# RWKV half step in another order: raw scores earlier, k and b scores a step ahead, substitution ahead of the k product

## The chip, the cores and the metric

The kernel runs on one core of one Trainium2 chip. The metric is the device time of one execution in microseconds; all times below are microseconds unless marked otherwise. TensorE multiplies, VectorE and ScalarE read its results out of PSUM, GpSimd works on SBUF alone, SP (SyncE) issues most DMAs.

## The reference, cut to what matters

One layer of a trunk over 128 context and 512 latent tokens: a norm, an input projection, RWKV-7 time mixing and gated linear attention in both directions, an output projection, a mixture of experts, a final norm. The change lies in RWKV alone:

```python
def rwkv_scan(r, w, k, a_vec, b_vec, v, s0, reverse):
    def step(S, inp):
        r_t, w_t, k_t, a_t, b_t, v_t = inp
        sa = jnp.einsum('bhvk,bhk->bhv', S, a_t)
        S = S * w_t[:, :, None, :] + sa[..., None] * b_t[:, :, None, :] + v_t[..., None] * k_t[:, :, None, :]
        return S, jnp.einsum('bhvk,bhk->bhv', S, r_t)
```

## The kernel before

The scan is done in chunks of 64 tokens. A step h is 128 tokens (two chunks, one on each half of the partitions) of one direction d, for 8 heads of 64; there are NS = 10 steps (five tiles of 128 tokens, two directions, p, d = divmod(h, 2)). Within a chunk the recurrence becomes a triangular system of 64x64 per head. Its inverse X is grown: the 8x8 blocks of the diagonal are inverted by substitution on GpSimd (`inverse_of_eights`), travel through DRAM to be spread over the partitions, and then three rounds on TensorE double them: Z = U X, then X grows by X^T Z (jobs Z8 and X16, Z16 and X32, Z32 and X64, each with a transposed X: X8t, X16t, X32t).

The work of a step is spread over four iterations of one loop, H = -3 to 9, written out by hand for every engine. An iteration (a half step) works on four steps at once, and this text keeps the names of the code: H itself (state work: WU, G, seq, Y), s = H+1 (the inversion), o = H+2 (factors of k and r), l = H+3 (raw scores L, whose blocks GpSimd inverts one iteration later). The jobs of TensorE in it:

- L(l): raw scores, 32 instructions of 64x64, copied out by ScalarE (`raw_blocks`), stored by SP (`blocks_out`). Needs VectorE's `a_and_b(l)`.
- k(s): scores of k, 32 instructions of 64x128, read out by VectorE (`masked_k`). Needs VectorE's `r_and_k(s)`, which needs GpSimd's `k_product(s)`, which needs ScalarE's `k_factors(s)`. b(s): scores of b, read out by VectorE (`masked_b`).
- tK, tB, tA: transposes, copied out by ScalarE. tB being done frees g.b for GpSimd's `b_product(l)`.
- Z8, X16, Z16, X32, Z32, X64: the rounds. Z and the transposed X are copied out by ScalarE, the X by VectorE (`grown`, a sum). AV: masked k scores times v (`scored_v`). `masked_a(s)` (VectorE) makes the three masked copies of the raw scores that the Z products read.
- WU(H) needs X64(H) summed; G(H) (`chunk_maps`) needs WU; seq and Y (`state_from_...`, `rows_from_...`) carry the state and make the output rows. Y is copied out by ScalarE (`first_rows`) for the first direction to reach a token tile, and added by VectorE (`added_rows`) for the second: steps 1, 6, 7, 8, 9.

Every engine takes its instructions in the order written. Three things order them across engines: semaphores of single steps; `filled`, which counts the jobs of TensorE; and the banks. There are NB = 8 banks of PSUM, and a job uses the bank of its number in the list `jobs` modulo 8. `open_bank` and `open_early` (lines 403 and 1912 to 1927) make TensorE wait until the job eight places earlier in the list is drained, that is, read out by VectorE or ScalarE; a pair of jobs (two banks) waits for both ahead of its first instruction, except WU and the transposes, which open one at a time. So the list fixes, besides the order, whose reader each job waits for.

The lines that matter: the list at 353 to 363; `b_product`, `k_product`, `inverse_of_eights` and their loop at 820 to 862; ScalarE's loop at 1149 to 1187; VectorE's at 1697 to 1732; TensorE's at 2447 to 2491. In the profile all matmuls have line 1907, all transposes 1911, all of ScalarE's operations 907; VectorE's lines are 1558 (`masked_a`), 1573 (`masked_k`), 1566 (`masked_b`), 1582 (`grown`), 1590 and 1591 (chunk maps), 1536 and 1539 (`a_and_b`), 1544 to 1549 (`r_and_k`), 1600 (`next_state`), 1611 (`added_rows`).

## Time and profile before

| | us |
|---|---|
| median of 3 runs | 1030.03 |
| lowest, highest | 1026.69, 1031.54 |
| the profiled execution | 1028.65 |
| its span | 1026.8 |

| engine | busy us | share of the span |
|---|---|---|
| TensorE, matmul | 882.8 | 86% |
| TensorE, weight load | 543.9 | 53% |
| VectorE | 578.1 | 56% |
| ScalarE | 312.3 | 30% |
| GpSimd | 144.9 | 14% |

The span is from the first to the last instruction; the execution's own time is 1.85 longer. Weight loads overlap matmuls, so the two TensorE rows don't add. The granted TensorE clock is 0.92 of full speed in the mean. The loop of half steps runs from about 437 to 684; the start of it (half steps -3 to 0) is bound by waits from engine to engine, from then on TensorE is busy most of the time.

### The profile page before, as it was taken

The page shows a single profiled execution, that of the slowest core. Times are in us where ns is not written, and L with a number is a line of the kernel's source. Part 1 is how long each engine was busy: PE and PEld are TensorE (multiplying, and loading weights), DVE is VectorE, ACT ScalarE, POOL GpSimd, SP SyncE. Part 2 cuts the span into 40 slices and gives each one's busy share as a digit, 9 for nine tenths or more (in the row PEclk, how much of TensorE's full clock was granted, in tenths as well). Part 3 has the DMA queues.
Part 4 walks back from the last instruction along what each step waited for, and adds up shares of the span by engine and source line. Part 5 has one row for each costly group of instructions (what it writes and reads, how often), then busy time and mean ns, then how long its engine had stood idle before and what let it go on. Part 6 is the DMA issues. An engine that isn't in the chain of part 4 may idle for free.

```text
span 1026.8 us, 21484 instructions
## 1 busy us (share of the span) xinstructions
PE 882.8 (86%) x8900; PEld 543.9 (53%) x8900; DVE 578.1 (56%) x968; ACT 312.3 (30%) x549; POOL 144.9 (14%) x295
## 2 busy tenths in 40 slices
PE   2799999996995899625988898889995799999996
PEld 0545455563653555425877787754565544444442
DVE  1524026689799268863655666578535144445457
ACT  3221110131000216464655665323121022232213
POOL 6000111103002000042333224000000110010031
PEclk9799999997998789658999999999995699999998
DMA  9800522222223230002121221196005679999957
GB/s 341 312 34 1 177 82 93 83 83 82 83 97 128 83 92 1 1 14 50 32 41 31 42 40 33 47 309 229 41 21 182 228 260 366 363 374 367 341 142 226
DMA packets 119760, 142.46 MB, mean 139 GB/s; under 512 B 49964, under 2 KB 85224, under 8 KB 119272
## 3 DMA queue, kind: packets, MB, share of 16 engines
q1 hardware_dynamic: 110824, 116.55, 34.6%
q0 software_dynamic: 3744, 13.63, 4.3%
q10 hardware_dynamic: 5088, 10.82, 2.8%
q8 instruction: 74, 1.21, 0.5%
q14 instruction: 30, 0.25, 0.1%
HBM read 122.99 MB, written 18.00 MB: 137 GB/s over the span
## 4 chain that ended last, share of the span: by engine, by line
PE 74%; DVE 14%; issue 5%; ACT 2%; DMA 2%; POOL 1%; SPq 1%; ACTq 0%; DVEq 0%; POOLq 0%
PE bank L1907 67%; PE bank L1911 7%; DVE rk_r L1354 3%; DMA region<-in_w_ada_dram 1%; ACT region L907 1%; DMA rk_r<-h_rows_dram,slot_tokens 1%; DVE region L1354 1%; DVE cl_b L1256 1%; POOL yg_b L814 1%; DVE vtok_b L1465 1%; DVE cl_b L1825 1%; DVE region L1896 0%; ACT ada_row_buffers L907 0%; ACT w_sb L907 0%; DVE kk_b L1463 0%
## 5 line engine op out<-in xcount | busy, mean ns | idle before, releaser
L1907 PE MATMUL bank<-region 64*64 64x64 f32 (+3 forms) x3904 | 406.4, 303 | 45.6 <-issue 29.2
L1907 PEld LDWEIGHTS bank<-region 64*64 64x64 f32 (+1 forms) x3904 | 236.1, 152 | 203.7 <-issue 189.8
L907 ACT ACTIVATE region<-bank 128x256 f32<-128x256 f32 (+3 forms) x216 | 97.9, 453 | 409.4 <-PE bank L1907 290.4
L1911 PE MATMUL bank<-ident,region 128*128 128x128 f32 (+2 forms) x403 | 69.8, 310 | 27.3 <-DMA scratch<-in_gla_gk_dram 12.6
L1907 PE MATMUL bank<-region,rk_r 128*128 128x512 f32 x176 | 80.1, 610 | 0.8 <-issue 0.8
L1911 PEld LDWEIGHTS bank<-ident,region 128*128 128x128 f32 (+2 forms) x403 | 51.4, 158 | 44.4 <-issue 28.1
L1877 DVE TENSOR_SCALAR region<-region 128x256 f32<-128x256 f32 x16 | 4.7, 294 | 100.4 <-ACT region L907 100.4
L1354 DVE SCALAR_TENSOR_TENSOR rk_r<-region,vec,rk_r 128x512 f32<-128x512 f32 x64 | 54.2, 847 | 2.3
L1907 PEld LDWEIGHTS bank<-region,rk_r 128*128 128x128 f32 x176 | 33.6, 196 | 39.7 <-issue 38.5
L1582 DVE TENSOR_TENSOR region<-bank,region 128x256 f32<-128x256 f32 x60 | 25.5, 425 | 47.6 <-PE bank L1907 46.3
L882 POOL DMA_INDIRECT rk_r<-h_rows_dram,slot_tokens x16 | 15.2, 949 | 245.3 <-PE bank L1911 131.9
L1907 PE MATMUL bank<-scratch,region 64*64 64x64 f32 (+1 forms) x688 | 42.9, 230 | 4.8 <-DVE region L1591 2.9
L1907 PE MATMUL bank<-vtok_b,region 64*64 64x64 f32 x928 | 43.5, 218 | 2.7 <-DVE region L1611 1.6
L1907 PE MATMUL bank<-region,scratch 64*64 64x128 f32 (+1 forms) x512 | 37.3, 425 | 7.2 <-DMA region<-in_w_ada_dram 6.4
L1907 PEld LDWEIGHTS bank<-scratch,region 64*64 64x64 f32 (+1 forms) x688 | 40.3, 143 | 5.0 <-issue 3.9
L828 POOL TENSOR_TENSOR region<-kk_b,region 128x512 f32<-128x512 f32 x10 | 12.9, 1288 | 212.6 <-DVE region L1694 103.8
L1907 PEld LDWEIGHTS bank<-vtok_b,region 64*64 64x64 f32 x928 | 40.3, 135 | 4.4 <-issue 2.6
L907 ACT ACTIVATE region<-region 128x256 f32<-128x256 f32 (+1 forms) x27 | 24.7, 915 | 44.7 <-DVE region L1371 43.9
L1907 PE MATMUL bank<-cl_b,ada_row_buffers 128*128 128x512 f32 x80 | 35.3, 594 | 0.1
L1907 PE MATMUL bank<-cl_b,rk_r 128*128 128x512 f32 x80 | 35.2, 592 | 0.0
L1907 PE MATMUL bank<-rk_r,ada_row_buffers 128*128 128x512 f32 x80 | 35.1, 592 | 0.0
L1277 DVE COPY ada_row_buffers<-bank 128x512 f32<-128x512 f32 x12 | 8.3, 691 | 44.7 <-PE bank L1907 44.5
(282 smaller groups left out, 1152.4 us busy)
## 6 DMA issues: line engine op xcount, KB each, us to landing
region<-in_moe_w_dram SPq DMA_DIRECT2D x38, 1024.0 KB, 10.0
region<-in_w_ada_dram SPq DMA_DIRECT2D x12, 2048.0 KB, 8.9
region<-in_w_in_dram SPq DMA_DIRECT2D x6, 2048.0 KB, 7.8
cl_b<-in_moe_w_dram SPq DMA_DIRECT2D x10, 1024.0 KB, 12.5
expert_rows_dram<-yg_b ACTq DMA_DIRECT2D x14, 512.0 KB, 6.9
region<-late_condition_dram SPq DMA_DIRECT2D x3, 1024.0 KB, 9.3
a_rows_dram<-region SPq DMA_DIRECT2D x20, 128.0 KB, 3.0
region<-inverse_rows_dram SPq DMA_DIRECT2D x20, 128.0 KB, 3.2
```

The source lines that it names most:

```text
L814: tell(pool.tensor_tensor(yg_b[:, :], yg_b[:, :], sgm, ALU.mult), s_sig)
L828: tell(pool.tensor_tensor(g.b, kkT[:, :, tok], aa[:, d, :, tok], ALU.mult), s_t1)
L882: pool.indirect_dma_start(out=xg[:, i % 3], out_offset=None, in_=h2_dram, in_offset=bass.IndirectOffsetOnAxis(ap=idx[:, e:e + 1], axis=0)) ...
L907: return act.activation(out, in_, func, **kw)
L1256: own(dve.tensor_tensor_scan(u, scanm[:, :], u, 0.0, ALU.mult, ALU.add))
L1277: out_of(dve.tensor_copy(adarow(n), bank(("ada", n))[:, :]), "ada", n)
L1354: own(STT(out, lat[:, i:i + GH, j:j + GW], tap(i, j), out, ALU.mult, ALU.add))
L1465: tell(STT(prod[:, i], rT[:, i], vec[:, vrk + i:vrk + i + 1], kT[:, i], ALU.mult, ALU.mult), s_bon)
L1582: out_of(TT(dst[:, hp::2], bank((n, h, hp))[:, 0:RC * HD].rearrange("p (h i) -> p h i", h=RC), src[:, hp::2], ALU.add), n, h, hp)
L1825: tell(STT(acc[:, t], x1[:, t], rstd[:, t:t + 1], fg, ALU.mult, ALU.mult), s_yout)
L1907: return pe.matmul(out, lhsT, rhs, start=start, stop=stop)
L1911: return pe.transpose(out, in_, ident[0:n, 0:n])
```

## The change

Four edits, all of order. No instruction is added or removed; the same products, masks, copies and DMAs are issued.

- TensorE: L(l) moves from behind Z32 to behind Y, ahead of X32. k and b are computed one iteration earlier, for o in place of s, between Z32 and X64. X8t goes ahead of Z8, and tB between Z8 and G.
- The list of jobs follows, so every job's bank and the job it waits for change.
- ScalarE's copies follow TensorE's order: tK ahead of WU, X8t ahead of Z8, L ahead of AV. `k_factors(o)` moves from the head of the iteration to behind Z16.
- GpSimd: `inverse_of_eights(o)` ahead of `k_product(o)`. VectorE: in iteration 1 alone `added_rows` goes ahead of X32's sum; its order is otherwise the same.

```diff
@@ the list of jobs
-            jobs += inside(s, pair("k", s)) + inside(H, pair("WU", H))
-            jobs += inside(s, [("tK", s)] + pair("b", s) + pair("Z8", s) + [("X8t", s)]) + inside(H, pair("G", H)) + last(H, "G")
-            jobs += inside(s, [("tB", s), ("tA", s)] + pair("X16", s) + pair("Z16", s)) + inside(H, [("seq", H, 0)])
-            jobs += inside(H if H < NS - 2 else -1, [("seq", H, 1)]) + inside(s, [("X16t", s)]) + inside(H, pair("Y", H))
+            o = H + 2
+            jobs += inside(s, [("tK", s)]) + inside(H, pair("WU", H))
+            jobs += inside(s, [("X8t", s)] + pair("Z8", s) + [("tB", s)]) + inside(H, pair("G", H)) + last(H, "G")
+            jobs += inside(s, [("tA", s)] + pair("X16", s) + pair("Z16", s)) + inside(H, [("seq", H, 0)])
+            jobs += inside(H if H < NS - 2 else -1, [("seq", H, 1)]) + inside(s, [("X16t", s)]) + inside(H, pair("Y", H)) + inside(l, pair("L", l))
             if H == 1:
                 jobs += [("st", 0), ("st", 1), ("s0",), ("mrow",)]
-            jobs += inside(s, pair("X32", s) + [("AV", s), ("X32t", s)] + pair("Z32", s)) + inside(l, pair("L", l)) + inside(s, pair("X64", s)) + last(s, "X64")
+            jobs += inside(s, pair("X32", s) + [("AV", s), ("X32t", s)] + pair("Z32", s)) + inside(o, pair("k", o) + pair("b", o)) + inside(s, pair("X64", s)) + last(s, "X64")
@@ GpSimd
                 if 0 <= H + 2 < NS:
+                    inverse_of_eights(H + 2)
                     k_product(H + 2)
-                    inverse_of_eights(H + 2)
@@ VectorE
+                if H == 1:
+                    added_rows(H)
                 if new:
                     grown("X32", s)
-                if back:
+                if back and H != 1:
                     added_rows(H)
@@ TensorE
                 if new:
-                    scores("k", s)
+                    turned("tK", s)
                 if back:
                     wu_rows(H)
                 if new:
-                    turned("tK", s)
-                    scores("b", s)
+                    turned_x("X8t", s)
                     times_u("Z8", s)
-                    turned_x("X8t", s)
+                    turned("tB", s)
...
                 if back:
                     rows_from_state(H)
+                if later:
+                    scores("L", l)
...
                     times_u("Z32", s)
-                if later:
-                    scores("L", l)
+                if next_:
+                    scores("k", o)
+                    scores("b", o)
                 if new:
                     grown("X64", s)
```

## Rows read from the trace of the kernel before

**Rows 1.** The page: busy time by engine, and the chain by engine.

```profile
PE 882.8 (86%) x8900; PEld 543.9 (53%) x8900; DVE 578.1 (56%) x968; ACT 312.3 (30%) x549; POOL 144.9 (14%) x295
...
PE 74%; DVE 14%; issue 5%; ACT 2%; DMA 2%; POOL 1%; SPq 1%; ACTq 0%; DVEq 0%; POOLq 0%
```

**Rows 2.** Stretches: from:to, length, busy of five engines, clock, DMA share, GB/s.

```profile
487.00:493.00 6.00, 6.00 (x161) 5.22 (x157) 2.21 (x6) 3.19 (x6) 1.80 (x2) 0.72 0.19 27
...
580.00:600.00 20.00, 17.95 (x598) 15.75 (x596) 12.13 (x23) 12.86 (x26) 6.61 (x19) 1.00 0.20 37
```

**Rows 3.** Timeline of TensorE, 584 to 615: start, length, what, count, [idle before].

```profile
584.06 0.69 PE L1907 MATMUL bank<-region,ada_row_buffers 64*64 64x64 f32 x32 [0.43 <-ACT ada_row_buffers L907]
...
586.41 1.16 PE L1907 MATMUL bank<-region 64*64 64x64 f32 x64
...
588.22 0.69 PE L1907 MATMUL bank<-region,ada_row_buffers 64*64 64x64 f32 x32 [0.65 <-ACT region L907]
...
590.13 2.31 PE L1907 MATMUL bank<-region 64*64 64x128 f32 x37 [0.39 <-issue]
592.36 0.66 PE L1911 MATMUL bank<-ident,region 128*128 128x128 f32 x4
592.95 1.16 PE L1907 MATMUL bank<-region 64*64 64x64 f32 x64
...
594.63 1.10 PE L1907 MATMUL bank<-region,scratch 64*64 64x128 f32 x32
...
598.86 0.63 PE L1907 MATMUL bank<-region 64*64 64x64 f32 x29
...
603.98 0.69 PE L1907 MATMUL bank<-region,w_sb 64*64 64x64 f32 x32 [0.43 <-ACT w_sb L907]
...
608.14 0.69 PE L1907 MATMUL bank<-region,w_sb 64*64 64x64 f32 x32 [0.64 <-ACT region L907]
...
614.22 1.10 PE L1907 MATMUL bank<-region,scratch 64*64 64x128 f32 x32
```

**Rows 4.** Timeline of VectorE over the same half step.

```profile
584.87 0.88 DVE L1582 TENSOR_TENSOR region<-bank,region 128x256 f32<-128x256 f32 x2 [1.92 <-PE bank L1907]
...
586.72 0.69 DVE L1549 TENSOR_TENSOR region<-region 128x512 f32<-128x512 f32 x1
589.02 0.88 DVE L1582 TENSOR_TENSOR region<-bank,region 128x256 f32<-128x256 f32 x2 [1.61 <-PE bank L1907]
589.94 1.76 DVE L1558 TENSOR_TENSOR region<-region,maskA 128x1536 f32<-128x1536 f32 x1
591.73 1.42 DVE L1573 TENSOR_TENSOR region<-bank,mask 128x512 f32<-128x512 f32 x2
593.76 0.88 DVE L1566 TENSOR_TENSOR region<-bank,mask 128x256 f32<-128x256 f32 x2 [0.62 <-PE bank L1907]
...
597.69 0.89 DVE L1582 TENSOR_TENSOR region<-bank,region 128x256 f32<-128x256 f32 x2
```

**Rows 5.** Timeline of ScalarE: X16t's copy, Z32's and L's copies, `k_factors`.

```profile
583.10 0.60 ACT L907 ACTIVATE ada_row_buffers<-bank 128x512 f32<-128x512 f32 x1 [2.92 <-PE bank L1911]
...
587.21 1.63 ACT L907 ACTIVATE region<-bank 128x256 f32<-128x256 f32 x4
588.88 2.08 ACT L907 ACTIVATE region<-region,small,vec 128x128 f32<-128x128 f32 x4
```

**Rows 6.** Timeline of VectorE in half step 6: `added_rows`.

```profile
626.19 0.88 DVE L1611 TENSOR_TENSOR region<-bank,region 128x256 f32<-128x256 f32 x2
```

**Rows 7.** Timeline of the loop's start: X32(0), last substitution for step 1, Z8(1), G(0).

```profile
475.20 0.69 PE L1907 MATMUL bank<-region,w_sb 64*64 64x64 f32 x32 [1.15 <-ACT region L907]
...
478.72 0.21 POOL L854 TENSOR_TENSOR ada_row_buffers<-ada_row_buffers,region 64x14 f32<-64x14 f32 x1
...
486.76 0.69 PE L1907 MATMUL bank<-region 64*64 64x64 f32 x32 [2.32 <-issue]
...
487.97 1.96 PE L1907 MATMUL bank<-region,scratch 64*64 64x128 f32 x32
```

More of the change, by code:

```diff
@@ L1151, in _ @@
                 back, new, next_, later = H >= 0, 0 <= s < NS, 0 <= o < NS, l < NS
-                if next_:
-                    k_factors(o)
+                if new:
+                    turned("tK", s)
                 if back:
@@ L1158, in _ @@
                 if new:
-                    turned("tK", s)
+                    turned_x("X8t", s)
+                    by_chunk("Z8", s)
                 if l == 1:
@@ L1164, in _ @@
                 if new:
-                    by_chunk("Z8", s)
-                    turned_x("X8t", s)
                     turned("tB", s)
@@ L1172, in _ @@
                     by_chunk("Z16", s)
+                if next_:
+                    k_factors(o)
+                if new:
                     turned_x("X16t", s)
@@ L1177, in _ @@
                     first_rows(H)
+                if later:
+                    raw_blocks(l)
                 if new:
@@ L1181, in _ @@
                     by_chunk("Z32", s)
-                if later:
-                    raw_blocks(l)
                 if s == NS - 1:
@@ L2447, in _ @@
             for H in range(-3, NS):
-                s, l = H + 1, H + 3
-                back, new, later = H >= 0, 0 <= s < NS, l < NS
+                s, o, l = H + 1, H + 2, H + 3
+                back, new, next_, later = H >= 0, 0 <= s < NS, 0 <= o < NS, l < NS
                 if new:
-                    scores("k", s)
+                    turned("tK", s)
                 if back:
@@ L2454, in _ @@
                 if new:
-                    turned("tK", s)
-                    scores("b", s)
+                    turned_x("X8t", s)
                     times_u("Z8", s)
-                    turned_x("X8t", s)
+                    turned("tB", s)
                 if back:
@@ L2463, in _ @@
                 if new:
-                    turned("tB", s)
                     turned("tA", s)
@@ L2478, in _ @@
                     rows_from_state(H)
+                if later:
+                    scores("L", l)
                 if H == 1:
@@ L2485, in _ @@
                     times_u("Z32", s)
-                if later:
-                    scores("L", l)
+                if next_:
+                    scores("k", o)
+                    scores("b", o)
                 if new:
```

## The prediction

> **What bounds the kernel now.** Read the page's busy table and its chain first: TensorE is busy 86% of the span and carries 74% of the chain that ended last [rows 1]. That is a mean over many stages, so read next the table of stretches, for the loop that the change touches (about 437 to 684 us): in a steady 20 us TensorE is busy 17.95, VectorE 12.13, ScalarE 12.86, GpSimd 6.61, at the full 2.4 GHz [rows 2]. TensorE leads, but 2 us are idle. Third, the timelines of TensorE and VectorE over one half step, which say who ends each idle time. With X32's start at 584.06 as zero, TensorE runs X32 0, Z32 and L together 2.35, X64 4.16, k, WU 6.07, tK 8.30, b and Z8 8.89, G 10.57, Z16 14.80, the next X32 19.92 [rows 3]. Its idle times are 0.43 ahead of X32 (ScalarE's copy of X16t), 0.65 ahead of X64 (ScalarE's copy of Z32) and 0.39 ahead of WU (VectorE's sum of X64) [rows 3]. The two that ScalarE ends are where the new order puts L, k and b. VectorE ends none of them but the last, so what must be read of it is how much time it has in hand where the new order puts a wait on it.
>
> The names: H is the half step's state work, s = H+1 the step being inverted, o = H+2, l = H+3.
>
> **Banks first.** Eight PSUM banks go round in the order of `jobs`, so a job waits until the job eight places earlier has been read out. I counted both lists. Before: Z8 takes over the banks of X64's second half and k's first, X8t that of k's second, tA and X16 those of b. After: WU's second half takes over the bank of k(o)'s first half, X8t that of k's second, and Z8 the two of b(o). k(o) and b(o) are read only by VectorE's `masked_k` and `masked_b`, and those stand where they stood, behind `grown("X64")` and `masked_a`. So k and b are computed earlier, but four banks stay shut until VectorE comes round, and TensorE now wants them at once.
>
> **Leg A, X32 to X64.** Removed: L (32 instructions). Added: k(o) and b(o). On full clock 32 instructions of 64x128 take 1.10 (G), of which some 0.05 overlap the next group: 1.05, and 32 of 64x64 take 0.55 (half of b and Z8) [rows 3]. k(o) needs `r_and_k(o)`, which VectorE runs behind X32's sum: it starts at 0.81 and the last product ends at 3.35 [rows 4]. Z32 would be over at 2.9, so k(o) waits, a new wait of 0.6. The hop from VectorE to TensorE is 0.23 from X64's sum (589.90) to WU and 0.28 from X16's (598.58) to Z16 [rows 3, 4]; the profile has none shorter than that among these, I take 0.2 as both have a bank to open besides. k at 3.55, b at 4.60, X64 at 5.15, where it stood at 4.16: +1.0. ScalarE's copy of Z32 (first at 3.15, now perhaps 0.8 later as L's two copies come ahead, four copies 1.63 [rows 5]) is done by 4.0, so the 0.65 does go, but under work and a wait that are longer. Bounds: 0.9 to 1.2.
>
> **Leg B, X64 to G.** Counted from X64's start at 588.22: its sum starts at 0.80, `masked_a` (1.76) at 1.72, `masked_k` (2 x 0.7) ends at 4.93, `masked_b` (0.88) no longer waits for TensorE and ends at 5.83 [rows 4]. TensorE: tK to 1.15, then idle until X64's sum, WU's first half 1.9 to 2.8, then idle until `masked_k`'s first half, about 4.35, WU's second half to 5.25, X8t to 5.85, Z8 when b's banks are free, 5.98, tB 6.53, G 7.12. Before it is 6.41 here and 6.08 two half steps on [rows 3]: +0.7 to +1.05, I take +0.9. This is also where k's old cover is missed: k had filled VectorE's time at X64's sum, of which only 0.39 showed.
>
> **Leg C, G to Z16.** Now 4.23, and already VectorE's: its four chunk-map operations and X16's sum end at 598.58, Z16 starts at 598.86 [rows 3, 4]. Moving tB ahead of G takes 0.55 from under this chain and so shortens nothing; at best the 0.3 behind the sum shrinks. -0.1, bounds -0.3 to 0.
>
> **Leg D, Z16 to X32.** L is now in front of X32: +0.55, and it covers X16t's copy: -0.43. +0.1. L's inputs (`a_and_b`) are ready long before in both orders.
>
> **GpSimd, SP, ScalarE.** Substitution ahead of the k product releases the inverse's store and loads one product earlier. In steady steps nobody waits for it: the inverse is in well before Z8. The k product now comes behind the substitution, but `b_product` starts earlier too, as tB does; by these shifts it ends about 2 us before `r_and_k` needs it. ScalarE's `k_factors` (4 x 0.52, 2.08) moves into an idle time of 2.92 ahead of X16t's copy [rows 5]. The queues of DMAs on SP keep their order; L's store goes a little earlier. All of this I cost at nothing in steady steps, with the bound of 0.5 a step if k's product is late.
>
> **Sum.** An ordinary half step: 1.0 + 0.9 - 0.1 + 0.1 = 1.9 longer, 22.2 for 20.3. Where the Y rows are summed by VectorE (two operations, 0.92 with their gap [rows 6]) ahead of `r_and_k`, leg A grows by that: 2.8. The H's in turn, each as the change at its X64:
> - H=-1: little lies between Z16 and X16t's copy there, so `k_factors` delays it, X32 by some 0.5 (475.20 now [rows 7]), and leg A adds 1.0: +1.5.
> - H=0: TensorE now stands 2.32 until the inverse lands at 486.76, 7.8 after the substitution's last operation ended [rows 7]. The inverse comes earlier, but Z8 at 475.7 + 5.15 + 5.98 = 486.8 is no earlier: VectorE takes the inverse's place. G stays at 488. Now the clock stood at 0.72 in the mean just there, G taking 1.96 for 1.10 [rows 2, 3, 7]; with the pause broken up, I let it stay high: -1.3 (bounds -1.6 to 0). Then D +0.1, and A with `condition_columns` ahead of `r_and_k`: +1.65. Together +0.5.
> - H=1: B, C, and D without a gap to cover (+0.55), A +0.7 as X32 to X64 is already longer there: +2.0.
> - H=2 to 5: 4 x 1.9 = 7.6. H=6 and 7: 2 x 2.8 = 5.6. H=8 has B and C alone: +0.8. H=9: nothing.
> 1.5 - 1.5 (swallowed by the 2.32) + 0.5 + 2.0 + 7.6 + 5.6 + 0.8 = 16.5. Behind the loop all shifts by it. The profiled execution took 1028.65 (its span 1026.8); 1045.2, so 1045. The median of the three runs lies 1.4 above that execution, which would make 1046.5; both lie well inside the range. By the legs' bounds (each -0.4 to +0.5 in seven half steps, start and clock -3 to +4) it is 1038 to 1053.
>
> **The rivals.**
> (1) The clock. The new waits break TensorE's work from X64 to Z8 into pieces: of about 5.3 some 2.3 are idle. Before, the 2.32 of idle ahead of 486.76 was followed by half clock (1.2 GHz) at a mean of 0.72 in the next 6 us, G taking 0.86 longer; with as much for the two transposes behind it I put a fall at 1.6 [rows 2, 3, 7]. If that came in each of 8 half steps: 8 x 1.6 = 13 more, 1058; in one or two, it is inside the forecast. For it: the sum of idle is the same. Against: it's in two pieces with WU between. The Trainium skill has this case (TensorE: Matmul & The Clock Gate, A second HAM failure mode: psum-queue depth-cycling): a kernel that cycles through PSUM banks idles shortly and often, and the clock swings. By that page it would be the 1058. The trace of before, with short waits in every half step at full clock [rows 2, 3], speaks against it so far.
> (2) Not slower: TensorE's order decides after all. If `masked_k` and `masked_b` were through before TensorE asks (the point: `masked_k`'s first half by 2.8 behind X64, where I have 4.2), the two gaps of 0.43 and 0.65 go in eight half steps, 8.6, and the clock's 1.3: 1019. VectorE's fixed 0.88 and 1.76 stand against it.
> (3) Between: the work in hand eats leg A but not leg B, 1.1 of gaps against 0.9 of bank waits, and the result is no change, 1029. It needs `r_and_k` 1 us earlier; its place behind X32's sum is fixed by the program.
>
> **How the numbers follow.** Forecast 1045 with 0.67, rival 1 with 0.16, rival 2 with 0.09, rival 3 with 0.08. A measurement of this kernel tells about 0.5% (5 us) from no change. Faster 0.09; same 0.08; slower 0.83. The range must leave out no more than 0.2: 1033 to 1058 leaves out the low rivals and little above.
>
> **What would show it.** After: X32 to X64 5.1 to 5.2, and k(o)'s group starting just behind L1549; no idle ended by ScalarE ahead of X32 and X64; two new idle times of TensorE behind X64, before each half of WU, 0.7 and 1.5; `masked_b` with no idle before it; VectorE idle less behind X64; masked_a to masked_a 22.2 in place of 20.2 to 20.5, 23 where rows are summed. It would be wrong if WU's halves follow each other (then banks don't bind), or if k starts right at Z32's end.

## The result, and the profile after

The changed kernel takes 1049.15 us (median of four runs, 1047.59 to 1051.12) where the kernel before took 1029.18 (median of four): a ratio of 1.0195, 95% interval 1.0163 to 1.0227. That is 20 us slower; the forecast was 1045, its range 1033 to 1058.

The page of the kernel after: busy time by engine, and the chain by engine.

```profile
PE 895.0 (85%) x8900; PEld 552.8 (53%) x8900; DVE 575.7 (55%) x968; ACT 312.4 (30%) x549; POOL 146.7 (14%) x295
...
PE 72%; DVE 16%; issue 3%; ACT 3%; DMA 3%; POOL 1%; SPq 1%; ACTq 0%; DVEq 0%; POOLq 0%
```

Against [rows 1]: the same 8900 matmuls are busy 12.2 us longer, and the chain gives VectorE 2 points more and TensorE 2 fewer. Now TensorE over the half step that answers to [rows 3] (start, length, what, count, idle time before and who ended it; X32 starts at 591.72).

```profile
591.72 0.69 PE L1912 MATMUL bank<-region,ada_row_buffers 64*64 64x64 f32 x32
593.62 1.15 PE L1912 MATMUL bank<-vtok_b,region 64*64 64x64 f32 x32 [1.21 <-DVE region L1585]
594.70 0.66 PE L1916 MATMUL bank<-ident,region 128*128 128x128 f32 x4
595.29 2.13 PE L1912 MATMUL bank<-region 64*64 64x64 f32 x96
597.42 0.69 PE L1912 MATMUL bank<-region,ada_row_buffers 64*64 64x64 f32 x32
598.05 0.66 PE L1916 MATMUL bank<-ident,region 128*128 128x128 f32 x4
599.22 1.09 PE L1912 MATMUL bank<-region 64*64 64x128 f32 x16 [0.51 <-DVE region L1585]
601.68 1.09 PE L1912 MATMUL bank<-region 64*64 64x128 f32 x16 [1.38 <-DVE region L1576]
602.71 0.66 PE L1916 MATMUL bank<-ident,region 128*128 128x128 f32 x4
603.42 0.69 PE L1912 MATMUL bank<-region 64*64 64x64 f32 x32
604.04 0.66 PE L1916 MATMUL bank<-ident,region 128*128 128x128 f32 x4
604.63 1.10 PE L1912 MATMUL bank<-region,scratch 64*64 64x128 f32 x32
```

X32 and X64 find their operands: no idle time ahead of either is ended by ScalarE here (in the last two half steps, which have no L, it still is: 0.43 and 1.32, 0.43 and 1.11). Behind X64 stand two idle times, 0.51 where the rows of before have 0.39, and a new one of 1.38; WU, one group of 32 before, comes in halves of 16, and the second waits for line 1576, `masked_k`. VectorE beside it, to be held against [rows 4]:

```profile
598.23 0.88 DVE L1585 TENSOR_TENSOR region<-bank,region 128x256 f32<-128x256 f32 x2 [3.17 <-PE bank L1912]
599.15 1.76 DVE L1561 TENSOR_TENSOR region<-region,maskA 128x1536 f32<-128x1536 f32 x1
600.94 1.42 DVE L1576 TENSOR_TENSOR region<-bank,mask 128x512 f32<-128x512 f32 x2
602.39 0.88 DVE L1569 TENSOR_TENSOR region<-bank,mask 128x256 f32<-128x256 f32 x2
605.85 0.43 DVE L1593 TENSOR_TENSOR region<-bank,identh 128x256 f32<-128x256 f32 x1 [2.58 <-PE bank L1912]
```

X64's sum, `masked_a`, `masked_k` and `masked_b` follow without a gap, and the second half of WU starts at 601.68, just as the first of `masked_k`'s two operations has ended (600.94 + 0.71). Then VectorE idles 2.58 for G.

In this half step AV came late, so k found its operands. Two half steps earlier it waited, 0.41; the trace names nobody, but line 1552, the last product of `r_and_k`, ends at 548.86, 0.10 ahead:

```profile
548.17 0.69 DVE L1552 TENSOR_TENSOR region<-region 128x512 f32<-128x512 f32 x1
548.96 1.57 PE L1912 MATMUL bank<-region 64*64 64x128 f32 x64 [0.41 <-issue]
```

**The ledger.** VectorE's sums mark the legs in every half step: A from X32's sum to X64's, B from X64's to the first chunk map, C to X16's, D to X32's. Between the first X64's sum and the tenth, nine steps:

| us | before | after | change |
|---|---|---|---|
| A, nine legs | 39.4 | 53.1 | +13.8 |
| B | 65.0 | 75.5 | +10.6 |
| C | 17.1 | 16.5 | -0.6 |
| D | 69.8 | 68.3 | -1.5 |
| nine steps | 191.2 | 213.4 | +22.2 |
| first X64's sum at | 480.2 | 478.1 | -2.1 |
| behind the tenth | 355.4 | 356.7 | +1.3 |

The three last rows make 21.4, the difference of the two profiled executions (1050.10 and 1028.65). The -2.1 is not the change's doing. GpSimd's first product of the loop, ahead of which the two kernels are the same, starts 2.8 earlier in the profiled execution after; from there to the first X64's sum it is 42.8 before and 43.5 after.

```profile
437.38 1.27 POOL L828 TENSOR_TENSOR region<-kk_b,region 128x512 f32<-128x512 f32 x1 [103.75 <-DVE region L1694]
434.62 1.27 POOL L829 TENSOR_TENSOR region<-kk_b,region 128x512 f32<-128x512 f32 x1 [103.67 <-DVE region L1697]
```

Leg B has two lengths. It is 6.48 in most half steps before; after, it is 7.62 at H = 2, 3, 5 and 7, and 9.0 at H = 0, 1, 4, 6 and 8. The second length is the clock. Of H = 4:

```profile
575.01 1.09 PE L1912 MATMUL bank<-region 64*64 64x128 f32 x16 [0.51 <-DVE region L1585]
577.48 1.97 PE L1912 MATMUL bank<-region 64*64 64x128 f32 x16 [1.38 <-DVE region L1576]
579.38 1.11 PE L1916 MATMUL bank<-ident,region 128*128 128x128 f32 x4
```

and in the table of stretches (clock behind the five busy times), this fall and the one of H = 6:

```profile
577.40:580.80 3.40, 3.32 (x32) 2.66 (x36) 1.56 (x4) 0.81 (x2) 0.00 (x0) 0.50 0.00 0
625.20:628.60 3.40, 3.40 (x51) 2.62 (x46) 1.11 (x3) 1.20 (x2) 0.00 (x0) 0.50 0.00 0
```

The idle times are the same 0.51 and 1.38 as at H = 5 above, but the second half of WU then runs at 1.2 GHz, 1.97 for 1.09, and the fall costs 9.0 - 7.62, about 1.36 of leg. Before, the loop had one fall (a stretch at a granted clock of 0.50) from 488.0 to 491.5 [rows 2]; after, five in these nine steps. So leg B's +10.6 is nine times 1.14 and five times 1.36, 17.1, less 6.6 by which four of its nine places had been longer than 6.48 before (9.86 at H = 0, with the wait for the inverse and the fall, and 8.93 at H = 8, with a pause of 2.06 of which more below).

### The profile page after: what moved, and what is told of

It is laid out like the page before. It is cut to its first block, busy times and chain, and to the rows that moved or that the text cites. A ratio compares the mean times of both kernels' runs of the same rounds, so it can differ in the third digit from the quotient of the medians.

```text
span 1048.3 us, 21494 instructions
## 1 busy us (share of the span) xinstructions
PE 895.0 (85%) x8900; PEld 552.8 (53%) x8900; DVE 575.7 (55%) x968; ACT 312.4 (30%) x549; POOL 146.7 (14%) x295
## 3 DMA queue, kind: packets, MB, share of 16 engines
q8 instruction: 74, 1.21, 0.5%
## 4 chain that ended last, share of the span: by engine, by line
PE 72%; DVE 16%; issue 3%; ACT 3%; DMA 3%; POOL 1%; SPq 1%; ACTq 0%; DVEq 0%; POOLq 0%
PE bank L1912 66%; PE bank L1916 7%; DVE rk_r L1357 3%; ACT region L908 2%; DVE region L1561 2%; DMA region<-in_w_ada_dram 1%; DVE region L1585 1%; DMA rk_r<-h_rows_dram,slot_tokens 1%; DVE region L1576 1%; DVE region L1357 1%; DVE cl_b L1259 1%; POOL yg_b L815 1%; DVE vtok_b L1468 1%; DVE cl_b L1830 0%; DVE region L1901 0%
## 5 line engine op out<-in xcount | busy, mean ns | idle before, releaser
L1912 PE MATMUL bank<-region 64*64 64x64 f32 (+3 forms) x3904 | 411.5, 309 | 60.1 <-issue 19.4
L1912 PEld LDWEIGHTS bank<-region 64*64 64x64 f32 (+1 forms) x3904 | 240.3, 156 | 222.6 <-issue 179.9
L1916 PE MATMUL bank<-ident,region 128*128 128x128 f32 (+2 forms) x403 | 73.4, 315 | 27.7 <-DMA scratch<-in_gla_gk_dram 12.7
L829 POOL TENSOR_TENSOR region<-kk_b,region 128x512 f32<-128x512 f32 x10 | 12.9, 1290 | 226.4 <-PE bank L1916 111.8
L1280 DVE COPY ada_row_buffers<-bank 128x512 f32<-128x512 f32 x12 | 8.3, 691 | 43.7 <-PE bank L1912 43.5
## 6 DMA issues: line engine op xcount, KB each, us to landing
region<-in_moe_w_dram SPq DMA_DIRECT2D x38, 1024.0 KB, 10.1
```

What stands on the lines that cost most here:

```text
L829: tell(pool.tensor_tensor(g.b, kkT[:, :, tok], aa[:, d, :, tok], ALU.mult), s_t1)
L1912: return pe.matmul(out, lhsT, rhs, start=start, stop=stop)
L1916: return pe.transpose(out, in_, ident[0:n, 0:n])
```

## The experiments

Each was read by its legs, by the waits of TensorE, and by its falls of the clock. "Stops" is TensorE's idle time in the nine steps that nothing in the trace ends ("issue" in the view of waits); what most of them are comes with the fourth group of runs.

| kernel | us | ratio to before, 95% | first X64's sum at | nine steps | falls in them | stops |
|---|---|---|---|---|---|---|
| before | 1028.2 to 1029.2 | | 480.2 | 191.2 | 1 | 12.9 |
| after | 1049.15 | 1.0195 (1.0163, 1.0227) | 478.1 | 213.4 | 5 | 8.7 |
| a_masks_early | 1039.91 | 1.0109 (1.0083, 1.0135) | 479.5 | 200.6 | 2 | 14.7 |
| a_rk_early | 1045.05 | 1.0175 (1.0156, 1.0194) | 482.2 | 202.8 | 1 | 6.6 |
| a_both_early | 1036.40 | 1.0076 (1.0047, 1.0104) | 484.8 | 194.6 | 2 | 10.2 |
| a_wu_twice | 1038.72 | 1.0103 (1.0058, 1.0148) | 478.9 | 200.8 | 1 | 6.8 |
| a_L_back | 1044.35 | 1.0158 (1.0118, 1.0199) | 483.1 | 203.5 | 0 | 10.5 |
| a_both_L_back | 1034.24 | 1.0059 (1.0035, 1.0082) | 481.4 | 197.4 | 2 | 13.1 |
| a_pool_undone | 1068.61 | 1.0393 (1.0355, 1.0430) | 483.7 | 225.7 | 7 | 8.0 |
| b_L_first | 1035.00 | 1.0068 (1.0045, 1.0090) | 480.0 | 197.6 | 2 | 12.0 |
| b_best | 1029.83 | 1.0005 (0.9989, 1.0021) | 481.0 | 191.9 | 1 | 16.7 |
| b_shift | 1025.78 | 0.9975 (0.9953, 0.9998) | 479.5 | 188.9 | 1 | 10.1 |
| b_tk | 1026.00 | 0.9982 (0.9962, 1.0002) | 480.4 | 185.7 | 0 | 12.0 |
| b_tk_rk | 1024.26 | 0.9955 (0.9933, 0.9978) | 478.6 | 187.0 | 0 | 12.8 |

The columns behind the ratio are of one execution each, and two of them carry a spread that is not the edits'. GpSimd's first product of the loop starts anywhere from 434.6 to 439.2, though all these kernels are the same up to there, and the first X64's sum moves with it. And the mean granted clock of the executions that make up a median differs as much as the falls could make it: 0.915 to 0.922 in the kernel after (the profiled one had 0.915), 0.917 to 0.927 in a_L_back (the profiled one 0.927), where five falls of 3.4 us at half clock are 0.008. How many falls the other executions had isn't known.

Stops counts short handovers between groups too, k's waits for `r_and_k` where the trace names nobody, and in the kernel before the 2.32 at 486.76 [rows 7], which was a wait for the inverse; the pauses in the middle of a group or over 0.25 that are none of these come to 5.4 there.

### The banks and `r_and_k`

```diff
 a_masks_early, against after (VectorE)
-    masked_a(s); masked_k(s); masked_b(s)
+    masked_a(s)
 ...
     r_and_k(o)
+    masked_k(o)
     grown("X64", s)
+    masked_b(o)
```

> The kernel after, with VectorE's masked_k of the next half step put ahead of X64's sum and its masked_b right behind that sum, so that WU's second half finds its bank read. Theory 1 (the banks cost leg B its 1.14 us per half step, and the idle that they break up costs the clock, 1.36 us in five half steps): leg B back to 6.5 us, the idle of 1.4 us before WU's second half gone, X64's sum later by at most 0.2; with nine half steps 8 to 10 us from the banks, and up to 7 more if no stretch of the loop falls to 1.2 GHz that did not fall before the change: 1033 us, between 1031 and 1041. Theory 2 (the clock falls for another reason, such as the waits of leg A): the 8 to 10 us from the banks alone, 1040, with the low clock still in five half steps. Theory 3 (the banks are not what is waited for: the order of TensorE itself costs the time): unchanged at 1049.

Measured 1039.9. What TensorE waited for in the nine steps, after and here (total, times, longest):

```profile
PE bank L1912 <- DVE region L1576: 12.4, 9, 1.4
PE bank L1912 <- DVE region L1585: 9.6, 17, 1.2
PE bank L1912 <- issue: 7.9, 13, 1.5
```

```profile
PE bank L1913 <- issue: 13.9, 27, 2.0
PE bank L1913 <- DVE region L1585: 9.3, 13, 0.9
PE bank L1913 <- ACT region L908: 7.0, 5, 2.3
PE bank L1917 <- issue: 0.8, 5, 0.2
```

The wait for `masked_k` was 9 x 1.38 = 12.4 and is gone; leg B is 6.13 in seven of its nine places, and only one fall stands behind an X64, at H = 7 (the other comes at 523.1 in leg A of H = 1). Theory 3 is out: the banks were waited for. Nine legs B give 75.5 - 56.6 = 18.9 back, yet the nine steps are only 12.8 shorter, as legs A and D got 6.1 longer and the stops rose from 8.7 to 14.7. In the medians 9.2 is left, half of what the banks, and the falls behind them, had cost in leg B. The time fits theory 1's upper end and theory 2's 1040 alike; what speaks for theory 1 is the falls, two for five, in one execution.

```diff
 a_rk_early, against after
 VectorE:  added_rows(1) / r_and_k(o) / X32's sum / other added_rows
 ScalarE:  k_factors(o) / growths_for_k(o) / X16t's copy
```

> The kernel after, with r_and_k of the next half step ahead of X32's sum on VectorE and the factor growths_for_k ahead of the copy of X16t on ScalarE, so that k's scores of the next half step don't wait for r_and_k. X32's sum can start later for it. Theory 1 (k's wait for r_and_k is 0.6 us of leg A, and 1.5 to 2.5 where added_rows or condition_columns stand ahead of it): the legs A of 4.95 to 5.1 fall to about 4.5, those of 5.7 to 7.5 to about 4.7; 6 to 8 us in all, 1042. Theory 2 (leg A is longer because TensorE has k's and b's scores in it, and r_and_k ends in time anyway): leg A stays at 5.0 and the time within 0.3% of the kernel after, 1049. Should r_and_k come too late for its new place, X32's sum waits for it and leg D grows by 0.5 or more: above 1049.

Measured 1045.05, 0.4% under the kernel after and between the two theories' 1042 and 1049. Where nothing else came in, leg A is 4.30 to 4.33 for 4.93 to 4.99: k's wait for `r_and_k` was 0.6 with its hop. Where it comes early, X32's sum waits for it: leg D is 7.62 nearly everywhere, and it was 7.0 in its shortest places. Theory 1 held for leg A; what it left out is that leg D pays the same 0.6. The nine steps are 10.7 shorter (7.0 in legs A, mostly at H = 0, 4, 6 and 7, and 5.5 in legs B, four falls fewer, against 1.8 more in D), but they begin 4.1 later; 2.1 of that lie ahead of the loop.

> Both edits in one: r_and_k ahead of X32's sum, masked_k ahead of X64's, masked_b behind it. If the two costs are separate (the banks on leg B, r_and_k on leg A) the gains add up: about 23 us less than the kernel after where the clock holds too, 1026 to 1030, level with the kernel before or a little under it; 1034 if the clock still falls in five half steps. If TensorE's order itself has a cost that no order of the other engines takes away, it ends above 1035 with the clock high.

Measured 1036.4. That is over the 1035 named for a cost of TensorE's order itself, but the clock fell twice. The best of its steps are 20.43 to 20.61, in TensorE's new order; the kernel before has 19.92 to 20.49. It lies 7.6 above before in the medians (1028.75) and 7.8 in the profiled executions. Of these, 4.7 are ahead of the first X64's sum, 1.0 of it ahead of the loop; between there and the sum the clock came up at 482.2 and not at 471.0 (the loop starts at 1.2 GHz in all of these kernels). 3.4 are in the nine steps, 2.4 of them in the one of H = 1, where AV waits 2.3 (below).

### The clock

```diff
 a_wu_twice, against after (TensorE): WU's first half is computed twice
+    for again in range(2 if j == 0 and h + 1 < NS else 1):
         for n in range(4 * j, 4 * j + 4):
```

> The kernel after, in which TensorE computes WU's first half twice while it waits for the bank of WU's second half (the repeated products are the same, nothing of the computation is left out). Sixteen more products of 64 rows take about 1.1 us, the idle ahead of the second half is 1.4. Theory 1 (the idle broken in two between X64 and Z8 is what makes the clock fall in five half steps): with the second idle filled, the loop's falls at this place go, 1.36 us each, and the time is about 1043 us; where the repeated products end after the bank is free they cost up to 0.2 each. Theory 2 (the falls hang on something else in the half step, such as the waits for r_and_k and the code loads): falls and time as in the kernel after, 1049 to 1051.

Measured 1038.7: work added, and 10.4 us gone. Leg B is 7.62 or 7.63 in six of nine places and long (9.69) only at H = 3, where the one fall of the nine steps stands, right behind a stop of 1.61; the kernel after had five. That agrees with the link: with TensorE at work between X64 and Z8 the falls went. But the edit also moves all later code, and it isn't only falls that went. The nine steps are 12.7 shorter: 4.3 in legs B (four falls of 1.36 are 5.4), 5.0 in legs A and 3.4 in legs D, which this edit doesn't touch and whose stops fell otherwise (s = 7: 5.85 for 7.52). The start and what lies behind take 2.1 back.

But the idle behind X64 isn't enough for a fall. a_rk_early (one fall) and a_L_back (none) keep all nine waits of 1.38; what they changed is work and waits in leg A. So what TensorE did in leg A bears on the clock too: four different removals of idle from the half step (k's wait for `r_and_k`, the same wait filled by L, the bank's wait filled by work, the bank's wait itself) each went with fewer falls, in the one execution that was profiled. That may in part be the execution and not the edit (see the granted clocks above), so what sets off a fall is not shown; neither is why in the kernel after it fell at H = 0, 1, 4, 6, 8 and not at H = 2, 3, 5, 7.

### The parts alone

```diff
 a_L_back, against after: L of half step l behind Z32 again, ahead of k(o) and b(o)
```

> The kernel after with the raw scores L back behind Z32, ahead of k and b of the next half step; all else as in the kernel after. Theory 1 (the loss is in k's and b's place: read late by masked_k and masked_b, clock and all): L's return changes little, 1046 to 1050 us; at H=1, where L's copy stood behind the context's copies (AV waited 2.3 us), up to 2 us come back; leg A gets L's 0.8 us, but k's group finds r_and_k's result then, so leg A is 5.2 to 5.3 and leg D shorter by 0.7. Theory 2 (L's move carries a good part of the loss): under 1042.

```profile
547.89 2.90 PE L1912 MATMUL bank<-region 64*64 64x64 f32 x128
550.70 0.69 PE L1912 MATMUL bank<-region,ada_row_buffers 64*64 64x64 f32 x32
```

Measured 1044.35. Z32, L, k and b run as one group of 128 without a gap: L fills the time in which k had waited for `r_and_k`. Leg A is 4.95 and 5.15 at H = 1 and 2 and 4.93 to 4.99 without L, so L in leg A costs 0.0 to 0.2 there; the other legs A hold stops or sums of rows. The time lies between the two theories' (1046 to 1050, under 1042): L's return gave 3.2 at H = 1 (23.59 for 26.75), and the profiled execution has none of the five falls, 6.8, while it begins 5.0 later. Of these 5.0, 4.6 lie ahead of the loop, so they are chance, and its granted clock was the highest of its four executions: the medians' 4.8 is the safer price.

```diff
 b_L_first, against before: L ahead of X32 (TensorE, ScalarE and the list of jobs), added_rows(1) ahead of X32's sum
```

> The kernel before with L's move alone (ahead of X32; added_rows of H=1 ahead of X32's sum as in the change). Theory 1 (leg A loses what leg D wins and the context's copies of H=1 delay AV by 2 us): 1029 to 1031 us, leg A 3.4, leg D longer by 0.7. Theory 2 (L's move is worth something by itself, since it fills a wait of leg D): 1024 to 1027. Theory 3 (it is a loss of its own): 1033 or more.

Measured 1035.0: a loss of 0.7% by itself, theory 3. TensorE's idle times around it:

```profile
524.19 1.15 PE L1909 MATMUL bank<-vtok_b,region 64*64 64x64 f32 x32 [2.28 <-ACT region L907]
...
572.94 0.69 PE L1909 MATMUL bank<-region,w_sb 64*64 64x64 f32 x32 [1.11 <-ACT region L907]
```

With L gone from leg A, X64 waits 1.11 for ScalarE's copy of Z32 where it had waited 0.65 [rows 3], and leg A stays at 4.16 in steady steps: L had been free there. At H = 1, AV waits 2.28 for its bank, since ScalarE copies L only behind the four copies of the context's rows and states, and a second fall stands right behind (525.3); legs D and A of that step take 18.3 for 15.9, 2.5 of the 6.4 by which the nine steps are longer. Of the rest, 2.8 are in the legs A of H = 4, 5 and 6 (stops of 1.13 and 0.97 in the first two) and 1.5 in other legs D.

```diff
 a_both_L_back, against after: a_both_early and a_L_back in one
```

> The kernel after with r_and_k ahead of X32's sum, masked_k ahead of X64's and masked_b behind it, and L back behind Z32: the move of k and b alone, without its two waits and without L's move. Theory 1 (what is left of the loss with both waits gone is L's move and the stops for code): leg A 5.0 to 5.3, B 6.13, C 1.84, D 7.1 to 7.6 as r_and_k is ahead of X32's sum; 20.2 to 20.6 per half step, H=1 without its 2.3 us behind the context's copies: 1029 to 1034. Theory 2 (L's move takes nothing once its copies don't collide, and its return adds 0.8 to leg A): 1037 or more.

Measured 1034.2, just over theory 1's range. H = 1 takes 22.94 for a_both_early's 26.53, as expected; but leg A is over 5.9 in five of its nine places, where 5.0 to 5.3 was forecast, and stops are 13.1. So the change without L's move and rid of both waits still costs 0.6%, 5.6 us. Which of its parts that is (k and b in leg A, `r_and_k` ahead of X32's sum, the places of X8t and tB, or where the stops fall) no run separates. L's move costs 6.8 by itself in b_L_first and 2.2 on top of this kernel (1036.4 for 1034.2, a difference within their spread), so the parts don't add up.

```diff
 a_pool_undone, against after (GpSimd)
-    inverse_of_eights(H + 2); k_product(H + 2)
+    k_product(H + 2); inverse_of_eights(H + 2)
```

> The kernel after with GpSimd's order as before: k_product, then the substitution. Theory 1 (GpSimd is beside the path, as the prediction had it): the ratio to the kernel after is 1 within 0.3%, 1047 to 1052 us. Theory 2 (k_product two microseconds earlier brings r_and_k, and so k's scores, forward): legs A of the half steps in which r_and_k waits for k_product shorten, 1043 to 1046; the substitution, later by one product, is not read until X8t, a leg further on, unless that is what is late at the loop's start, where it costs up to 1.3.

Measured 1068.6: both theories missed it, by 17 us. GpSimd's queue (line 834 is the k product, line 855 the substitution's last operation), and TensorE where it waits for the inverse:

```profile
580.00 1.28 POOL L834 TENSOR_TENSOR region<-region,rk_r 128x512 f32<-128x512 f32 x1 [7.18 <-ACT region L908]
...
586.60 0.21 POOL L855 TENSOR_TENSOR ada_row_buffers<-ada_row_buffers,region 64x14 f32<-64x14 f32 x1
```

```profile
593.61 1.11 PE L1916 MATMUL bank<-ident,region 128*128 128x128 f32 x4 [1.48 <-DMA region<-inverse_rows_dram]
```

The k product waits 7.18 for ScalarE, since `k_factors` now stands behind Z16's copy, and the substitution queues behind it. It ends at 586.8, its rows are back from memory at 593.6, and X8t waits for them: 7.5 us in seven of nine steps, six of nine legs B are 9.7 to 11.9, and of the seven falls in the nine steps five are twice as long as those of the kernel after (6.8). GpSimd's swap isn't an ornament beside the path: by these waits it pays for `k_factors`' move on ScalarE, though no run has that move taken back. It is worth something at the loop's start as well: from GpSimd's first product to the first X16's sum it is 34.5 here, 34.3 in the kernel before and 31.3 in the kernel after.

### The stops, and other orders with k and b in their old place

```diff
 b_shift, against before (TensorE)
+    if H == -2:
+        for _ in range(128):
+            pe.wait_ge(s_ab, 1)
```

> The kernel before with 128 repeated waits (on an event long past) put on TensorE's queue ahead of L(1), where the engine has 12.9 us without work. They do nothing but shift all later instructions of the loop by 128 in the instruction stream. TensorE's stops of 0.3 to 2.1 us in the middle of a group, ended by nothing that the trace names, stand in the kernel before at 516.38, 539.94, 560.67, 573.77, 619.53, 627.90 and 656.51 us. Theory 1 (they are waits for the next 16384 bytes of TensorE's code, which land on the instruction queue 1.3 to 1.5 us before each stop ends): the stops move to other instructions by half the distance between two loads (about 2.2 us), and with them the legs that are long; the sum changes by up to 3 us either way: 1026 to 1032. Theory 2 (they come from the work itself, so a bank or an operand late by a semaphore that the trace leaves out): stops at the same products as before, time equal within 0.2%.

In the kernel before, and in this one, TensorE's timeline with stops:

```profile
516.38 0.28 PE L1907 MATMUL bank<-scratch,region 64*64 64x64 f32 x2 [1.08 <-issue]
...
539.94 0.21 PE L1907 MATMUL bank<-vtok_b,region 64*64 64x64 f32 x1 [0.70 <-issue]
...
656.51 0.46 PE L1907 MATMUL bank<-region 64*64 64x64 f32 x17 [2.06 <-issue]
```

```profile
558.03 0.27 PE L1907 MATMUL bank<-vtok_b,region 64*64 64x64 f32 x1 [1.07 <-issue]
...
579.41 0.28 PE L1907 MATMUL bank<-scratch,region 64*64 64x64 f32 x2 [0.90 <-issue]
```

Of the seven stops of the kernel before, six are gone from their places in b_shift; the seventh (560.67, 0.37) has one of 1.07 close by, 3.7 behind X16's sum for 3.9. Others stand elsewhere, in a kernel whose loop is the same to the last instruction. Theory 2 is out. The view of the DMA queues from 513.5 to 516.5 of the kernel before holds one packet (40 slices of 75 ns):

```profile
GB/s 0 0 218 0 0 0 0 0 0 0 0 0 0 0 0 0 0 0 0 0 0 0 0 0 0 0 0 0 0 0 0 0 0 0 0 0 0 0 0 0
...
q8 instruction: 1, 0.02, 2.7%
```

It starts in the third slice and takes 0.027 x 16 x 3.0 = 1.3 us, to 515.0; the stop ends 1.4 later, at 516.38. All seven stops of before end 1.38 to 1.52 behind the end of such a load of 16384 bytes, five of the large ones in b_shift 1.34 to 1.51. These loads come every 4.1 us or so in the dense parts. A band 0.14 wide in 4.1 is not met seven times by chance, so such a stop is TensorE waiting for its code. The Trainium skill (Runtime: NRT & Kernel Launch, Instruction fetch mechanics) has code fetched in blocks of 16 KiB while the block before runs, and holds the fetch to be hidden by the pace of issue. The size agrees; that it is hidden doesn't hold in this loop, where TensorE loses 0.3 to 2.1 us at a stop. b_shift is 0.25% faster than before (0.9953 to 0.9998): where the loads fall is worth some 3 us (by the interval 0.2 to 4.8), at no change of work. Every edit to TensorE's order moves the loads too, so a difference of that size between two kernels here can't be put down to their order alone.

```diff
 b_best, against before: L ahead of X32; tK(o) between Z32 and X64; r_and_k(o) and added_rows(1)
 ahead of X32's sum; growths_for_k ahead of X16t's copy
```

> The kernel before, with three steps of its own kind: the raw scores L ahead of X32, the one transpose tK of the next half step between Z32 and X64 (k's and b's scores stay where they were), and r_and_k ahead of X32's sum. Theory 1 (TensorE work moved into the leg X32 to X64 costs only if its banks are read late or its operands come late, and here neither holds): leg B shortens by tK's 0.65 us, leg A changes by L's departure and tK's arrival to at most 4.2, leg D grows by 0.1: about 5 us less than before, 1024, between 1020 and 1029. Theory 2 (any order with L ahead of X32 lengthens X16 to X32 as much as it shortens the rest): 1029 to 1032.

Measured 1029.8, no change: theory 2's time. Leg B is 5.73 to 6.56 for 6.48 from H = 1 on, and leg A 4.05 to 4.07 at H = 0, 2 and 3, as theory 1 had it; but leg D is 7.7 to 8.8 from H = 2 to 7 (5.3 more in all nine), H = 1 has AV's wait of 2.3, and the stops are the highest of all, 16.7. Set beside b_tk below, the two things it took from the change on top of tK's move gave its gain away.

```diff
 b_tk, against before: tK(o) behind L, ahead of X64 (ScalarE's copy of it goes behind L's), and nothing else
     scores("L", l)
+    pe.wait_ge(s_rk, o + 1)
+    turned("tK", o)
     grown("X64", s)
```

> The kernel before with one step of TensorE moved, the transpose tK of the next half step, from ahead of b's scores to behind the raw scores L and ahead of X64; ScalarE's copy of it goes behind the copy of L. All else stays. Theory 1 (a step moved from leg B into leg A costs there only what stands over the cover of Z32's copy, and it has no bank that is read late): leg B 5.8 for 6.5, leg A 4.3 to 4.7 for 4.16 and up to 1 more at H=6 and 7, where r_and_k stands behind added_rows: 1 to 4 us less than before, 1025 to 1028. Theory 2 (leg A is full: everything put into it costs its whole length, and a stop for code comes more often the denser TensorE is): 1029 to 1033.

```profile
543.38 1.16 PE L1908 MATMUL bank<-region 64*64 64x64 f32 x64
544.48 0.65 PE L1912 MATMUL bank<-ident,region 128*128 128x128 f32 x4
545.08 0.79 PE L1908 MATMUL bank<-region,ada_row_buffers 64*64 64x64 f32 x32
```

tK's four transposes fill the 0.65 in which X64 waited for Z32's copy [rows 3]: leg A is 4.05 to 4.15 with it in the steady steps, not longer at all, and leg B 5.73 to 5.88 where no stop falls. The nine steps are 5.5 shorter and have no fall; the median of twelve runs is 1026.0, in theory 1's range, but by the ratio only 0.18% under before, with an interval that touches no change. b_shift, which moved nothing but code, has the same 1026 on the same chip: the legs show tK's gain, the final time doesn't yet.

> The kernel before with tK of the next half step behind the raw scores L, as in the run with that step alone, and VectorE's order around it set for it: r_and_k right behind X32's sum, ahead of added_rows and condition_columns; added_rows of H=1 ahead of X32's sum, since its bank is the one that AV waits for (1.61 us in the trace of the run with tK alone). Theory 1 (leg A is short of cover only where r_and_k stands behind other rows, 4.93 for 4.06 at three half steps and 4.85 at the loop's second; and AV's wait at H=1 is the order of VectorE): 2.5 us from the legs A and up to 1.6 at H=1, so 1022 to 1025 us, 0.4 to 0.6% under the kernel before. Theory 2 (the stops for code take back what the legs give): 1025 to 1028, as with tK alone.

This is b_tk with `r_and_k(o)` right behind X32's sum on VectorE, ahead of `added_rows` and `condition_columns`, and `added_rows` of H = 1 ahead of X32's sum.

Measured 1024.26, 0.9955 (0.9933 to 0.9978): faster than both kernels. The mechanism is only half borne out. AV's wait at H = 1 is gone (leg A 4.69 for 5.70), and legs A at s = 1 and 8 fell from 4.85 and 4.93 to 4.24 and 4.55; but at s = 7 leg A is 5.74 for 4.93, since `added_rows`, now later, holds a bank that TensorE wants (1.37 us), and stops fell on other places (1.14 for 0.64 in leg D of H = 1). Its nine steps are 1.3 longer than b_tk's in the profiled executions, and it is ahead only by starting them 1.7 earlier, all of it ahead of the loop. That its VectorE order adds to tK's move is therefore not shown. What is shown is that the two together, where their code loads happen to fall, are 0.2 to 0.7% faster than the kernel before.

## Why the prediction was right, point by point

**The sum.** 16.5 was forecast, 20.0 measured in medians and 21.4 in the profiled executions. The sign, the place and both mechanisms (the banks on leg B, `r_and_k` on leg A) were right. That the sum came so close is in part luck. Its terms for the nine steps make 15.0 and they took 22.2 more; the first X64's sum was to come 1.5 later and came 2.1 earlier, and 2.8 of those 3.6 lie ahead of the loop. The five falls, 6.8, are most of what the nine steps are over. (A small slip: with the bounds as given the low end is 1039, not 1038.)

**Banks first.** Right to the letter: WU comes in halves, its second waits for `masked_k`'s first operation, and `masked_b` has no idle time before it. X64 to G is 7.21 where 7.12 was worked out (597.42 to 604.63). The price of leg B was 0.9 and is 1.14: of the two lengths before, 6.08 and 6.41, the prediction took a middle, and the shorter is the steady one (it is the 6.48 between VectorE's marks; the 6.41 is 6.83 there). 7.21 - 6.08 is 1.13.

**Leg A.** 1.0 was forecast, 0.8 came in steps without a stop (4.93 to 4.99 for 4.16); k waited 0.4 and not 0.6, as X32's sum and Z32 lay closer to the forecast's upper ends. For H = 0 and 1, 1.65 and 0.7 were forecast, and 1.74 and 0.77 came; for H = 7, where rows are summed, 1.9 and 1.7. The nine legs came to 13.8, though, and the forecast to 10.2. Stops are most of the rest: 1.05 at 616.51 and 1.48 at 646.36, which nothing in the trace ends and which lie 1.41 and 1.33 behind a load, and probably 593.62, whose 1.21 stands in the first fence of TensorE under VectorE's name but ends 1.25 behind a load of code that landed at 592.37.

**Leg C and D.** C stayed at 1.83 (forecast -0.1). D was to grow by 0.1: its shortest is 7.00 with L ahead of X32 and 6.93 without (a_L_back). That it sums to -1.5 is at least in part the stops that the kernel before had in this leg (0.70, 1.08).

**The clock.** This step failed. The forecast let the clock stay high from H = 0 on and put 1.6 on a fall in the rival. A fall costs 1.36 and came in five half steps of the profiled execution, 6.8 of the 13 of rival 1. Against it I had set that the kernel before has short waits in each half step at full clock. That is true, and stops short of the question: before, these are 1.5 us in 20 in three pieces [rows 3] (a fourth, 0.42 ahead of seq, is in the trace but not in the rows, and VectorE ends it); after, 1.9 in the two between X64 and Z8 alone, with k's 0.4 shortly ahead. On the Trainium skill (TensorE: Matmul & The Clock Gate, A second HAM failure mode: psum-queue depth-cycling) the trace now agrees in kind: waits for banks, short and in each turn, and a clock that goes down and up. It was not every turn, and a_L_back's profiled execution shows the same bank waits with no fall.

**GpSimd at nothing.** Right for the steady steps of the change as it stands, with a wrong reason. Nobody waits for the substitution because the swap puts it ahead of a k product that waits for ScalarE. The prediction weighed each move alone (`k_factors` into an idle time of ScalarE, a swap on GpSimd) and bounded them at 0.5; the first without the second costs 19.5 us.

**The start.** 1.5 later was forecast for the first X64's sum, 0.5 of it for `k_factors` ahead of X16t's copy and 1.0 in leg A. Counted from GpSimd's first product it is 0.7, and that is a sum of larger terms. The first X16's sum comes 3.0 earlier (31.3 for 34.3), since the substitution no longer stands behind the k product, which the forecast put at nothing. From there to X32's sum it is 7.13 for 4.37, 2.8 and not 0.5 more, with L in front and X32 still waiting 2.79 for ScalarE where it had waited 1.15 [rows 7]:

```profile
471.78 1.14 PE L1912 MATMUL bank<-region,w_sb 64*64 64x64 f32 x32 [2.79 <-ACT w_sb L908]
```

**ScalarE's copies.** The forecast counted L's leaving as 0.55 less work in leg A. b_L_first shows it worth nothing there: X64 waits for ScalarE, and L was the cover. The 1.0 came out about right as k's wait took over that place.

**H = 1.** 2.0 was forecast and 2.58 came (26.75 for 24.17). Two terms were missing, the bank that ScalarE frees late, behind the context's copies (AV 2.27 for 1.6), and a fall, 1.36; leg D, 0.76 shorter for a stop less, hid part of them.

## What to carry to other kernels

In a ring of banks, count for each moved job who reads it and when: computing something earlier than its reader comes round shuts a bank for the jobs behind it, here 1.4 us per turn. A move into a leg is free only up to the idle time that it fills; the best one here moved 0.65 us of transposes into a wait of 0.65. When two queues are reordered together, price each without the other: one may be there to pay for the other. And before two profiles are set against each other, look at a mark ahead of the change: here one that no edit could move lay 4.6 us apart.

## What was not expected of the hardware

- TensorE waits for its own code. In this loop a load of 16384 bytes comes every 4.1 us or so, and stops of 0.3 to 2.1 us end about 1.45 behind the end of one; some 5.4 us of the nine steps in the kernel before. 128 idle instructions ahead of the loop moved six of seven.
- What a removed wait gives can be lost again: of 18.9 won in leg B by a_masks_early, 12.8 were left, with 14.7 us of idle time under "issue" for 8.7 in the kernel after. It isn't a rule: with `r_and_k`'s wait gone (a_rk_early) it is 6.6, with both 10.2. That data waits hide waits for code is therefore possible, not shown.
- Doing work twice made the kernel 10.4 us faster (1038.7 for 1049.15), about half of it where the clock stayed at 2.4 GHz and the rest in legs that the edit doesn't touch.
- The first X64's sum stands at 478.1 to 484.8 in these kernels, 6.7 us apart, as much as many of the edits are worth; 4.6 of that can come from ahead of the loop, where all are the same. The clock comes up at 464.8 to 482.2, and latest where the sum is latest, but not in the same order otherwise (466.9 goes with 482.2, 471.9 with 479.5).
